# Experts' rows summed on TensorE with diagonal matrices, together with turned attention products, a start by tiles and another order of loads

## The reference

```
for x in (context, latent):
    sh1, sc1, g1, sh2, sc2, g2 = ada_modulation(cond, w_ada, b_ada)        # silu(cond) @ w_ada
    h = rms_norm(x, norm1_g) * (1 + sc1) + sh1
    q, k, v, u_pool, u_conv = input_projection(h, w_in)
    a = attention(q, k, v)     # latent: 8 x 16 neighbourhood with a bias, and 256 cached keys, one softmax
    m = concat(a, multiscale_pool(u_pool), conformer_conv(u_conv))
    x = x + g1 * (m @ w_out)
    h2 = rms_norm(x, norm2_g) * (1 + sc2) + sh2
    x = x + g2 * grouped_moe(h2)   # 16 experts of 1024 -> 512 -> 1024, two for each token, weighted and summed
    y = rms_norm(x, final_g)
```

## Time and profile before

| | us |
|---|---|
| median of three runs | 750.83 |
| the three runs | 750.67, 753.99, 750.83 |
| the profiled execution | 752.79 |
| its span, first to last instruction | 750.9 |
| PE busy | 673.5 (90%) |
| DVE, ACT, POOL busy | 226.1, 159.3, 151.2 |
| mean granted clock of TensorE | 0.964 |

### The profile page before, as it was taken

The page is one execution under the profiler, slowest core; times in us unless marked ns, Lnnn a source line. Parts: engine busy times, 40 slices in busy tenths (PEclk is TensorE's granted clock), DMA queues, the critical chain, the costliest instruction groups (busy, mean ns, idle before and its releaser), DMA issues.

```text
span 750.9 us, 11852 instructions
## 1 busy us (share of the span) xinstructions
PE 673.5 (90%) x4923; PEld 412.1 (55%) x4923; DVE 226.1 (30%) x505; ACT 159.3 (21%) x330; POOL 151.2 (20%) x186
## 2 busy tenths in 40 slices
...
GB/s 249 385 271 128 242 225 1 347 332 175 1 122 390 190 115 2 0 292 184 65 301 70 282 358 326 383 275 400 380 390 392 417 360 412 407 410 176 45 288 131
DMA packets 50663, 186.17 MB, mean 248 GB/s; under 512 B 7152, under 2 KB 9577, under 8 KB 46384
## 3 DMA queue, kind: packets, MB, share of 16 engines
...
q10 hardware_dynamic: 112, 0.04, 0.0%
...
## 4 chain that ended last, share of the span: by engine, by line
PE 83%; DMA 6%; DVE 5%; SPq 2%; ACT 1%; issue 1%; POOL 1%; POOLq 0%; DVEq 0%; ACTq 0%
PE bank L1728 11%; PE bank L1735 10%; PE bank L1584 9%; PE bank L1465 7%; PE bank L1751 6%; PE bank L1760 5%; PE bank L1525 5%; PE bank L1412 4%; PE bank L1626 4%; DMA slots<-in_w_ada 3%; PE bank L1428 3%; PE bank L1743 3%; PE bank L1470 2%; PE bank L1715 2%; SPq L444 2%; DMA x<-in_x_prompt 2%
## 5 line engine op out<-in xcount | busy, mean ns | idle before, releaser
L1465 PE MATMUL bank<-ra,slots 128*128 128x512 f32 x192 | 83.3, 594 | 0.4 <-DVE ra L843 0.4
L1584 PE MATMUL bank<-slots,rc 128*128 128x512 f32 x160 | 69.9, 593 | 0.0
L1465 PEld LDWEIGHTS bank<-ra,slots 128*128 128x128 f32 x192 | 36.1, 190 | 45.6 <-issue 44.6
L1154 DVE TENSOR_TENSOR rc<-re,bank 128x256 f32<-128x256 f32 (+1 forms) x32 | 10.2, 359 | 160.8 <-PE bank L1735 88.5
L1353 POOL COPY gi<-ridx 128x1 uint32<-128x1 uint32 x18 | 3.6, 198 | 272.8 <-PE bank L1715 237.7
L1728 PE MATMUL bank<-rb,rc 128*128 128x512 f32 x128 | 56.2, 595 | 0.0
L858 DVE SCALAR_TENSOR_TENSOR re<-re,cwT 128x670 f32<-128x670 f32 x60 | 52.3, 945 | 0.0
L554 ACT ACTIVATE rb<-bank 128x512 f32<-128x512 f32 (+1 forms) x64 | 31.1, 525 | 94.7 <-PE bank L1465 49.6
L1584 PEld LDWEIGHTS bank<-slots,rc 128*128 128x128 f32 x160 | 29.9, 190 | 34.9 <-issue 34.9
L1735 PE MATMUL bank<-slots,rc 128*64 128x256 f32 x384 | 43.7, 382 | 0.0
L1241 POOL TENSOR_TENSOR mod<-mod,vecT 128x8 f32<-128x8 f32 (+1 forms) x8 | 19.6, 2455 | 117.9 <-ACT mod L554 117.9
...
## 6 DMA issues: line engine op xcount, KB each, us to landing
...
```

Source lines behind the costliest of these rows:

```text
L1465: ins = mm(b[:, :], w[:, k, m * P:(m + 1) * P], hT[:, k, 0:NLAT], start=k == 0, stop=k == KD - 1)
L1584: ins = mm(b[:, :], mT[:, k, i * P:(i + 1) * P], wo[k // 4][:, k % 4, 512 * hf:512 * hf + 512], start=k == 0, stop=k == KD - 1)
```

## The change

- **Start**: x_sample's tiles are two whole rows of the grid, loaded and stored as they lie; the copies into hT write with a stride to get the order by columns (`by_columns`). Only the identity is loaded ahead of x, the other constants after w_in's first part, which comes in two pieces. Sums of squares, roots and scalings go tile by tile, two of the sums on DVE; ada(0) stands between the transposes.
- **Zeros**: issued before the 14th load in place of the 13th.
- **Attention**: a loop over 16 pairs. DVE writes the biased scores back into the bank; ACT takes one exponential of 512 and its sum. v is the stationary operand, the transposed probabilities move, and two heads fill the halves of an output bank, already turned. DVE spreads the inverse sums over rows (`spread`), PE transposes them (R), DVE multiplies (`weigh`) into mT. Scores, PT and the rest have fixed banks. w_out's products start with the pooled and convolved half. POOL's writing of the modulation stands behind its loop.
- **Routing**: the counts ahead of a tile are summed on PE; each of the first two experts gets its list by itself, and POOL gathers by it without a copy. Fillers are 4, 12 and 4 long in place of 8, 18 and 8.
- **Tail**: DVE makes ten diagonal matrices from the weights. After the experts PE runs 36 fillers, then for each tile two products per half, weights times rows, into PSUM; DVE multiplies by g2 out of PSUM. `gate` and L1189 go. ACT loads the root's table earlier.

```diff
-PAIRS = 4 * H
+PAIRS = 2 * H
+ASIDE.update({("S", u): u % 4 for u in range(2 * PAIRS)})
+ASIDE.update({("PT", u): 4 + u % 2 for u in range(2 * PAIRS)})
...
-    def tile_rows(ap):
-
-        return ap.rearrange("(r i c) d -> i c r d", r=ROWS, i=TT - 1)
+    def by_columns(ap, i):
+
+        return ap.rearrange("p k (s r) -> p k r s", r=ROWS)[:, :, 2 * i:2 * i + 2]
+
+    def by_rows(ap, i):
+
+        return ap.rearrange("p m (r i c) -> p i m c r", r=ROWS, i=TT - 1)[:, i]
...
-        sp.dma_start(cst[:, :], t["consts"]).then_inc(S["cst_in"], 16)
+        sp.dma_start(cst[:, 0:P], t["consts"][:, 0:P]).then_inc(S["cst_in"], 16)
...
-                    sp.dma_start(x[:, i, :], tile_rows(t["x_sample"][0])[i]).then_inc(x_in[i], 16)
+                    sp.dma_start(x[:, i, :], t["x_sample"][0, i * P:(i + 1) * P]).then_inc(x_in[i], 16)
...
+            if n == 3:
+                sp.dma_start(cst[:, P:], t["consts"][:, P:]).then_inc(S["rest_in"], 16)
...
-            if n == 12:
+            if n == 13:
...
+            if key == ("in", 3):
+                sp.dma_start(dst[:, 0:2], src[:, 0:2]).then_inc(S["w3_in"], 16)
+                sp.dma_start(dst[:, 2:KD], src[:, 2:KD]).then_inc(w_slot[SLOT[n]], 16)
...
+        def square(i):
+            act.wait_ge(x_in[i], 16)
+            if i:
+                act.wait_ge(S["ssq_ready"], i // 2)
+            sc.activation(junk, x[:, i, :], ACT.Square, accum_out=ss[:, 0, i:i + 1]).then_inc(S["ssq_ready"], 1)
+        def root(i):
+            act.wait_ge(S["ms_ready"], i + 1)
+            sc.activation(ss[:, 1, i:i + 1], ss[:, 0, i:i + 1], ACT.Sqrt).then_inc(S["sqrt_ready"], 1)
+
+        square(0)
...
                 b = filled(act, "S", u)
-                nmx = st[:, 2, u:u + 1]
-                sc.activation(pr[:, u % 4, 0:256], pr[:, u % 4, 0:256], ACT.Exp, bias=nmx)
-                evac(pr[:, u % 4, 256:512], b[:, 256:512], ACT.Exp, bias=nmx)
+                if u >= 4:
+                    filled(act, "PT", u - 4)
+                evac(pr[:, u % 4, :], b[:, :], ACT.Exp, bias=st[:, 2, u:u + 1], accum_out=st[:, 0, u:u + 1])
...
+        def xT(i):
+            b = filled(dve, "xT", i, 1)
+            b = b[:, :].rearrange("p (k n) -> p k n", k=4)
+            if i < TT - 1:
+                evac(by_columns(hT[:, 4:8, 0:NLAT], i), b.rearrange("p k (r s) -> p k r s", r=2))
...
+        def mean_of(i):
+            if i % 2:
+                dve.wait_ge(x_in[i], 16)
+                link(v.tensor_tensor_reduce(rc[:, 4 * LP:4 * LP + D], x[:, i, :], x[:, i, :], 1.0, 0.0, ALU.mult, ALU.add,
+                                            ss[:, 0, i:i + 1]))
+            else:
...
+        def scaled(i):
+            dve.wait_ge(S["sqrt_ready"], i + 1)
+            link(v.reciprocal(ss[:, 2, i:i + 1], ss[:, 1, i:i + 1]))
...
+        def spread(tile):
+            emptied(dve, "S", 8 * tile + 7)
+            one = rw[:, 8 * tile:8 * tile + 8]
+            link(v.reciprocal(one, st[:, 0, 8 * tile:8 * tile + 8]))
...
+                filled(dve, "R", tile - 1)
+            v.tensor_copy(at.rearrange("p (h e) -> p h e", h=H),
+                          one.unsqueeze(2).to_broadcast([P, H, DH])).then_inc(S["spread_ready"], 1)
...
+        def weigh(tile):
+            dve.wait_ge(S["pv_done"], 4 * tile + 4)
+            b = filled(dve, "R", tile)
+            evac(at, b[:, :])
+            emptied(dve, "R", tile)
+            v.tensor_tensor(by_rows(mT[:, 0:4, 0:NLAT], tile),
+                            bank[6 + tile % 2][:, :].rearrange("p (m c r) -> p m c r", m=4, r=ROWS),
+                            at.rearrange("p (m c r) -> p m c r", m=4, r=ROWS), ALU.mult).then_inc(S["mixed_ready"], 1)
...
-        for i in range(STEPS):
-                b = filled(dve, "S", i)
-                dve.wait_ge(S["bm_ready"], i + 1)
-                link(v.tensor_tensor_reduce(pr[:, i % 4, 0:256], b[:, 0:256], bm[:, i % 4, :], 1.0, st[:, 0, i:i + 1],
-                                            ALU.add, ALU.max, st[:, 1, i:i + 1]))
-                v.tensor_scalar(st[:, 2, i:i + 1], st[:, 1, i:i + 1], -1.0, None, ALU.mult).then_inc(S["smax_done"], 1)
+        for j in range(STEPS):
+            for u in (2 * j, 2 * j + 1) if j < PAIRS else ():
+                link(v.tensor_reduce(st[:, 0, u:u + 1], b[:, 256:512], AX.X, ALU.max))
+                dve.wait_ge(S["bm_ready"], u + 1)
+                link(v.tensor_tensor_reduce(b[:, 0:256], b[:, 0:256], bm[:, u % 4, :], 1.0, st[:, 0, u:u + 1],
+                                            ALU.add, ALU.max, st[:, 1, u:u + 1]))
+                v.tensor_scalar(st[:, 2, u:u + 1], st[:, 1, u:u + 1], -1.0, None, ALU.mult).then_inc(S["smax_done"], 1)
+            if j >= 4 and j % 4 == 0:
+                spread(j // 4 - 1)
+            if j >= 5 and j % 4 == 1:
+                weigh(j // 4 - 1)
...
-        link(v.tensor_tensor(sel2, hot[:, 0], hot[:, 1], ALU.add))
-        v.memset(before[:, 0:NE], 0.0)
-        for c in range(1, TT):
-            ins = v.tensor_tensor(before[:, (c + 1) * NE:(c + 2) * NE], before[:, c * NE:(c + 1) * NE],
-                                  sel2[:, c * NE:(c + 1) * NE], ALU.add)
-            if c < TT - 1:
-                link(ins)
-        ins.then_inc(S["route_ready"], 1)
+        v.memset(sel2[:, n:n + NE], 0.0)
+        v.tensor_tensor(sel2[:, 0:n], hot[:, 0], hot[:, 1], ALU.add).then_inc(S["route_ready"], 1)
...
+        v.tensor_tensor(firsthot, three(sel2[:, 0:n])[:, :, 0:2], K("tok").unsqueeze(2).to_broadcast([P, TT, 2]),
+                        ALU.mult).then_inc(S["tiles_hot"], 1)
+        for e in range(2):
+            v.tensor_tensor(rowhot[:, e * TT:(e + 1) * TT, :], K("iota").unsqueeze(1).to_broadcast([P, TT, P]),
+                            three(rank)[:, :, e].unsqueeze(2).to_broadcast([P, TT, P]), ALU.is_equal).then_inc(S["rows_hot"], 1)
         pick(rk, three(rank))
-        v.tensor_tensor(firsthot.rearrange("p (k i) e -> p k i e", k=2),
-                        hot.rearrange("p k (i e) -> p k i e", i=TT)[:, :, :, 0:2],
-                        K("tok").unsqueeze(1).unsqueeze(3).to_broadcast([P, 2, TT, 2]), ALU.mult).then_inc(S["tiles_hot"], 1)
-        rows_of(rk)
+        b = filled(dve, "first", 0)
+        evac(ridx[:, 0:1], b[:, 0:1])
...
+        for b in range(2):
+            dve.wait_ge(h2_out[b], 16 * (3 - b))
+        v.tensor_tensor(diag, ident.unsqueeze(1).unsqueeze(1).to_broadcast([P, 2, TT, P]),
+                        wts[:, :, :].unsqueeze(3).to_broadcast([P, 2, TT, P]), ALU.mult).then_inc(S["diag_ready"], 1)
...
-            dve.wait_ge(S["first_ready"], c + 1)
-            link(v.scalar_tensor_tensor(fy[:, c, 0, :], fy[:, c, 1, :], wts[:, 1, c:c + 1], fy[:, c, 0, :],
-                                        ALU.mult, ALU.add))
             if c >= 1:
                 mean_square(c - 1)
-            link(v.tensor_tensor(fy[:, c, 0, :], fy[:, c, 0, :], bc[:, 0 if c < 4 else 1, :], ALU.mult))
+            for hf in range(2):
+                dve.wait_ge(S["sum_ready"], 2 * c + hf + 1)
+                cols = slice(512 * hf, 512 * hf + 512)
+                link(v.tensor_tensor(fy[:, c, 0, cols], bank[(2, 6)[c % 2] + hf][:, :], bc[:, 0 if c < 4 else 1, cols], ALU.mult))
...
-        def gate(c):
-            act.wait_ge(fy_in[c], 32)
-            sc.activation(fy[:, c, 0, :], fy[:, c, 0, :], ACT.Copy, scale=wts[:, 0, c:c + 1]).then_inc(S["first_ready"], 1)
-
-        gate(0)
-        gate(1)
+        sc.activation(ss[:, 1, 0:1], ss[:, 1, 0:1], ACT.Sqrt)
...
-            if s == 16:
-            if s == 22:
-                emptied(pool, "modT")
-                pool.dma_start(t["modr"], mrow).then_inc(S["mrow_out"], 16)
-            if s == 25:
-                pool.wait_ge(S["mrow_out"], 16)
-                for q, (vec, who) in enumerate(((0, 1), (0, 0), (2, 1), (1, 1))):
-                    pool.dma_start(bc[:, q, :], row(vec, who)).then_inc(S["bc_in"], 16)
+        emptied(pool, "modT")
...
-        gather(0, 0)
-        gather(1, 1)
+        for b in range(2):
+            emptied(pool, "first", b)
+            g.indirect_dma_start(xg[:, b, :], None, t["h2d"],
+                                 bass.IndirectOffsetOnAxis(ap=ridx[:, b:b + 1], axis=0)).then_inc(xg_in[b], 16)
...
-            ada(j)
-            adT(j)
+            if i == 2:
+                ada(0)
+        adT(0)
+        ada(2)
+        adT(2)
...
-            if hf == 0:
-                emptied(pe, "aT", i)
...
-            for k in range(KD):
+            for k in (4, 5, 6, 7, 0, 1, 2, 3):
+                if (i, hf, k) == (0, 0, 0):
+                    pe.wait_ge(S["mixed_ready"], 4)
+                if (i, hf, k) == (4, 0, 0):
+                    emptied(pe, "aT", 4)
                 ins = mm(b[:, :], mT[:, k, i * P:(i + 1) * P], wo[k // 4][:, k % 4, 512 * hf:512 * hf + 512],
-                         start=k == 0, stop=k == KD - 1)
+                         start=k == 4, stop=k == 3)
...
+        def score(pair):
```

(68 more changed lines are left out.)

287 lines of the change are left out of this document (142 added, 145 removed).

## The result

| | before | changed |
|---|---|---|
| median (us) | 751.13 (4 runs, 750.67 to 753.99) | 722.11 (4 runs, 721.50 to 722.42) |
| profiled execution, its span | 752.79, 750.9 | 721.98, 720.1 |
| PE busy | 673.5 | 682.2 |
| mean granted clock | 0.964 | 0.992 |

The account below looks back on a forecast made before the run. TensorE was taken as the bound, with 83% of the span on the last chain. Terms 8 + 7 + 11.5 + 2.5 + 3.5 = 32.5 off 752.8 gave 720.3, less 2.0 for the median 718.3 us; range 710 to 733.

Parts of the forecast that it names:

- Start, 8: Start up to w_in's first product: x in whole rows and roots tile by tile save 8 us, VectorE the longest queue.
- The next pieces of w_ada then arrive about when TensorE asks for them: Start, after w_in's first product: the following w_ada loads come about on time; no size given.
- a wait for w_ada before 40 us: Start: listed among the signs that would show the forecast wrong; no size given.
- Zeros, 7: At w_ada's columns 7: issuing ada(7) before the zeros removes the 4.84 us wait and slow product, 7 us less.
- Attention, 11.5: Attention's 16 pairs of heads: values stationary, two heads side by side, a pair 2.97 instead of 3.77 us; 11.5 us less.
- Routing, 2.5: Routing ahead of the experts: fewer small steps and shorter fillers, 2.5 us less, between 0 and 4.5, the clock low.
- nothing changes: Routing, from the first gather's issue to the first expert's product: stays at 8.0 us.
- Tail, 3.5: Tail after the experts: VectorE's period per tile falls from 5.03 to 4.03 us, 3.5 us less.
- no overlap: Rival in attention: two 64-wide groups take 106 ns a record, so attention gains nothing, 730 us; chance 0.12.
- The tail at the low clock: Rival in the tail: TensorE at 1.2 GHz from 718.6 on, last tile some 11 us later, 733 us; chance 0.10.
- The chain: Rival in attention: no two pairs overlap, 5.9 us a pair, 34 us more, kernel slower at 764 us; chance 0.04.
- The load decides the start: Rival at the start: the load sets it and ada(8) waits, 721 to 724 us; no chance of its own.

Follow-up runs that it names:

- e9: The changed kernel run again without an edit; 722.76 us, ratio 0.9606.
- e10: The changed kernel with the rest of the constants issued two places later, ahead of the sixth load instead of the fourth; 722.08 us.
- e12: The changed kernel with the constants two places later and the tail's last scaling of three tiles off VectorE, filler 36; 719.85 us.
- e2: The changed kernel with x_sample loaded and y_sample stored by columns again and plain copies into hT and mT; 726.61 us.
- e1: The changed kernel with the zeros issued before the 13th load again; 728.83 us.
- e7: The kernel before with one edit, the zeros issued before the 14th load; 745.29 us, ratio 0.9911.
- e4: The changed kernel without the 36 filler products ahead of the tail's products; 724.84 us.
- e6: The changed kernel with the routing's fillers of before, 8, 18 and 8 products in place of 4, 12 and 4; 722.66 us.
- e3: The changed kernel with the old tail: weighting on ScalarE, weighted sum on VectorE, no diagonal matrices, filler or early root table; 725.30 us.
- e9 to e12: Four runs of the changed kernel: unedited, constants later, and constants later with three last scalings off VectorE at filler 28 (719.63 us) or 36 (719.85).
- e5: The changed kernel with a pair's values in turn, eight records of one head, then eight of the other; 730.20 us.

## Why the prediction came out as it did

The sign, the order of the three large parts and the range were right: 32.5 us were forecast of the spans, 30.8 came. The time missed by 3.8 us, in two halves. **The offset:** the forecast took 2.0 off because the profiled execution of before lay that far above its median. That was scatter: medians of before in later runs are 751.4 to 751.9, so the profiled execution lay about 1.2 high and the median of three 0.8 low, and the changed kernel's profiled execution stands at its median (721.98 and 722.11). **The terms** make the other 1.7, and that this is so little is in part luck: the routing gave 2.2 more than its term, which covers most of what attention and the tail fell short.

1. *Start, 8.* 7.9 to w_in's first product; then 0.7 went back. The number is near, but the path is another than the forecast's. VectorE was done with its last scaling at 19.5, not 20.8, and TensorE then waited 1.46 for w_ada's columns 2: the load set the first product, and the two errors nearly cancel. In ten traces of this start columns 2 come 5.41 to 5.42 us behind the start of ada(0), as 2.1 MB at 387 GB/s do (the changed kernel's window from 17 to 27 us moves 390), wherever ada(0) stands. The forecast worked out the load only for x at 237 GB/s and not at the full rate. "The next pieces of w_ada then arrive about when TensorE asks for them" failed too: columns 1 came 0.6 late (1.5 in e9), behind the constants, and e10 and e12 show it. They set the second stage, which begins at 47.36 in e9 as well, though its first product came 0.9 sooner (27.06). The forecast had named a wait for w_ada before 40 us as a sign of being wrong, and it came. The load's price of 3 us that the rival gave is what e2 measured (3.1 to the first product, 3.9 behind it). The strided copies cost 1.1, just above the 1.05 allowed.
2. *Zeros, 7.* 6.8 in the two traces, 6.4 undone (e1), 7.0 made alone (e7). Right, ada(8) too: no wait in any run.
3. *Attention, 11.5.* 9.6. The term that was mis-sized is a record of the values: 56 ns estimated from two shapes, 64 measured. 0.12 us a pair, 1.9 us in sixteen, is as much as the miss. Another 0.9 went at the entry, where the first scores wait 0.83 for ScalarE's copy of a turned block, presumably since the scores' banks are now fixed, which no run tests; the forecast did not look at that place. w_out's order gave 0.5 back. TensorE had no other gap over a us: neither ScalarE nor VectorE became the bound.
4. *Routing, 2.5.* 4.7 in the traces. Ahead of the gather 3.1 were gained of the 3.5 expected. From the first gather's issue to the first expert's product "nothing changes" did not hold: 1.5 us went there in the changed kernel's trace, but only 0.2 in e9's of the same kernel (7.74 after 7.98), so the shorter fillers alone do not give it. From list to product twelve traces of this routing take 8.8 to 9.0 (six), 10.1 (four), 10.3 (e4) and 10.6 (e6, long fillers). The forecast's 2.5, taken for the low clock, is close to what an execution of the 10.1 gives (3.4); the profile is of one of the others.
5. *Tail, 3.5.* 2.2. VectorE's period came out at 4.01 for 4.03, so the mechanism is right. The term that was missing is the first tile: the forecast had its rows "at 718.6 as before", and they landed 1.5 us later after their gather; its end came 0.7 later still behind TensorE's products. Over the kernels this landing is 5.1 (before and e7), 5.4 (e3), 5.6 (e4), 5.7 (e2) and 6.6 to 6.8 (changed, e9 to e12). The four without a filler in the tail are the short ones, but e2 has the filler and 5.7, so the filler alone is not the cause, and it stays open.

The rivals: *no overlap* falls by e5, since the overlap is there and worth 7.8 us. The Trainium skill, page "TensorEngine Tiling (Array Packing)", section "Overview", under "Theoretical Speedup", promises up to twofold for a dimension of 64; here 106 ns became 64, a factor of 1.7, of which the alternation gives 1.5 (94 to 64 in e5). *The tail at the low clock* falls: the window after 692 is at 1.00 (below), and without filler (e4) the clock is back after four us; its price is 1.4, not 11. *The chain* falls: the waits in attention are 0.83, 0.42 and 0.78 us, once each. *The load decides the start* was right, at a price of 1.46 ahead of the first product and of 0.6 to 1.5 ahead of the second stage. The window of the changed kernel's tail, columns as in the earlier trace rows:

```profile
692.00:696.00 4.00, 3.87 (x9) 1.82 (x10) 0.75 (x2) 0.00 (x0) 3.09 (x4) 1.00 0.97 374
```
